# One decoder layer with attention, pooling and a 64-expert MoE: the per-layer projection takes the place of shared-expert products in the wait for the routing

## The reference, cut to what matters

```python
x = x + merged @ w_out
h2 = rmsnorm(x, g_ffn)
idx, wts = route(h2, w_router, router_bias)                  # 8 of 64 experts for a token
moe = routed_experts(h2, idx, wts, w_exp_gate, w_exp_up, w_exp_down) \
    + swiglu(h2, w_sh_gate, w_sh_up, w_sh_down)              # the shared expert, width 256
x = x + moe
ple_gate = sigmoid(rmsnorm(x, g_ple) @ w_ple_gate)
x = x + ple_gate * rmsnorm(p @ w_ple_proj, g_ple_post)       # p: 512 x 256, w_ple_proj: 256 x 1024
```

## Time and profile before

| | us |
|---|---|
| device time, median of 3 runs (lowest to highest) | 989.55 (988.99 to 990.61) |
| span of the profiled execution, first to last instruction | 986.4 |
| median less that span | 3.15 |
| PE busy / DVE / POOL / ACT in the span | 932.8 / 360.1 / 226.8 / 162.6 |
| PE: idle ahead of `up` / of `down`, in all | 26.1 / 3.1 |
| bytes moved by DMA, mean rate | 301.04 MB, 305 GB/s |

### The profile page before, as it was taken

How to read it: one execution, slowest core, us unless ns; L and a number is a source line. 1 busy time by engine, 2 the same in 40 slices (tenths; PEclk the granted TensorE clock), 3 DMA queues, 4 the chain that set the end, 5 groups by cost and what they waited for, 6 DMA issues and landing times.

```text
span 986.4 us, 15652 instructions
## 1 busy us (share of the span) xinstructions
PE 932.8 (95%) x6359; PEld 483.9 (49%) x6359; DVE 360.1 (37%) x773; ACT 162.6 (16%) x304; POOL 226.8 (23%) x344
## 2 busy tenths in 40 slices
PE   6999999999999999999999999989979889897798
PEld 4678788888655533333333333344323333332344
DVE  5565673336436733333332110111101111111687
ACT  2001324210011211111111111111101102121021
POOL 4115923162100112222222222212121211201110
PEclk9999999999999999999999999999989999999899
DMA  9940005421482699999999999999999999999972
GB/s 331 331 129 1 1 1 184 158 86 63 143 317 107 223 385 386 407 418 395 411 420 407 398 422 410 408 422 415 397 422 421 421 421 419 419 401 373 380 270 85
DMA packets 83912, 301.04 MB, mean 305 GB/s; under 512 B 9299, under 2 KB 35959, under 8 KB 59648
## 3 DMA queue, kind: packets, MB, share of 16 engines
q1 hardware_dynamic: 70144, 263.19, 67.8%
q0 software_dynamic: 11920, 33.63, 8.8%
q10 hardware_dynamic: 1776, 3.21, 0.9%
HBM read 279.26 MB, written 29.36 MB: 313 GB/s over the span
## 4 chain that ended last, share of the span: by engine, by line
PE 74%; DMA 20%; SPq 2%; DVE 2%; issue 1%; ACT 1%; POOL 0%; ACTq 0%; POOLq 0%
PE ps L2223 22%; DMA ring<-in_w_exp_up 18%; PE ps L1826 12%; PE ps L2252 8%; PE ps L1976 6%; PE ps L1955 5%; PE ps L2367 4%; PE ps L1782 3%; PE ps L1759 2%; PE ps L2047 1%; PE ps L1788 1%; DMA ring<-accumulator 1%; PE ps L2232 1%; DMA accumulator<-actT,stage 1%; SPq L525 1%; PE ps L1875 1%
## 5 line engine op out<-in xcount | busy, mean ns | idle before, releaser
L2223 PE MATMUL ps<-ring,gates 128*32 128x512 f32 x2560 | 289.3, 604 | 26.1 <-DMA ring<-in_w_exp_up 25.3
L2223 PEld LDWEIGHTS ps<-ring,gates 128*32 128x32 f32 x2560 | 88.8, 111 | 218.6 <-issue 217.7
L2252 PE MATMUL ps<-ring,poolbuf 128*32 128x512 f32 x1280 | 145.6, 595 | 3.1 <-DMA ring<-in_w_exp_down 3.1
L1573 DVE COPY poolbuf<-ps 128x256 f32<-128x256 f32 x40 | 17.0, 424 | 355.4 <-PE ps L2232 355.4
L791 POOL TENSOR_TENSOR tickets<-cst 128x1 f32<-128x1 f32 x77 | 14.5, 188 | 397.1 <-ACT actT L991 391.7
L2252 PEld LDWEIGHTS ps<-ring,poolbuf 128*32 128x32 f32 x1280 | 37.9, 109 | 83.5 <-issue 81.9
L991 ACT ACTIVATE actT<-ps,qT 128x1024 f32<-128x1024 f32 x40 | 44.5, 1113 | 142.3 <-PE ps L2252 142.3
L983 ACT ACTIVATE poolbuf<-ps 128x256 f32<-128x256 f32 x40 | 15.4, 384 | 280.0 <-PE ps L2223 280.0
L1826 PE MATMUL ps<-xrow,ring 128*128 128x256 f32 x256 | 57.9, 381 | 0.1
L1976 PE MATMUL ps<-ring,gates 128*128 128x512 f32 x128 | 56.4, 594 | 0.0
L1759 PE MATMUL ps<-cst,rows 128*128 128x128 f32 x352 | 47.6, 281 | 8.3 <-DVE rows L1087 8.3
(11 more groups left out here) (294 smaller groups left out, 1062.3 us busy)
## 6 DMA issues: line engine op xcount, KB each, us to landing
ring<-in_w_exp_down SPq DMA_DIRECT2D x64, 1024.0 KB, 17.6
ring<-in_w_exp_gate SPq DMA_DIRECT2D x62, 1024.0 KB
ring<-in_w_exp_up SPq DMA_DIRECT2D x62, 1024.0 KB
ring<-accumulator SPq DMA_DIRECT2D x12, 1024.0 KB, 13.1
ring<-in_w_gate SPq DMA_DIRECT2D x8, 1024.0 KB, 13.2
ring<-in_w_in SPq DMA_DIRECT2D x5, 1024.0 KB, 12.9
xrow<-in_x SPq DMA_DIRECT2D x8, 512.0 KB, 5.1
accumulator<-ring SPq DMA_DIRECT2D x1, 4096.0 KB, 19.9
```

Source lines behind the costliest of these rows:

```text
L2223: last = mm(bank(2 + k)[part, :], hgT[k][:, q, part], pair_view(EXPERT_SLOT[js[c]])[:, q], start=(q == 0), stop=(q == KD - 1))
L2252: last = mm(bank(6 + half)[part, :], eactT[r % 2][:, q, part], w[:, q, half * 512:(half + 1) * 512], start=(q == 0), stop=(q == 1))
```

## The change

1. `shared_up` is gone. In its places PE runs `ple_proj(m0, m1)`: the 16 products of 128x512 of `p @ w_ple_proj`, in the same pieces. They need six banks (`PLE_BANK`), and eight pairs of ACT instructions empty them: a copy to `pp` and a square with its sum (`ple_evict`).
2. The shared gate and up products of all four tiles are jobs: eight `late_T` and four `late_up` in steps 24 to 29, `shared_T` in 30, `shared_down` in 33 to 36. `ple_proj` and `ple_square` are no jobs any more; `ple_gain` (DVE, now from SBUF) is in steps 16 to 23.
3. The shared gate and up weights are loaded once, in four halves of 0.5 MiB. `w_ple_proj` is a dense unit in slot 8. Gate and up of expert 3 are loaded with the first experts, its down weights (slot 8) after the last `ple_proj`. `w_sh_down` is loaded in two halves after step 31.
4. `rows_T(0)`, `up(1)` and the first `silu` wait for `ple_squared`; `down(0)` and `up(1)` no longer wait for `shared_act`.

The core of the diff; renumbered jobs, the views of the buffers and `late_up`, whose body is as before but for the place of its weights, are left out.

```diff
@@ -54,9 +54,10 @@
-LATE = (2, 3)
+UPS = 3 * NT
...
-JOB_STEP = [SMALL_AT + n // 2 for n in range(8)] + [SMALL_AT + 6 + n // 2 for n in range(4 * NT)]
+JOB_STEP = [SMALL_AT + n // 2 for n in range(UPS + 2)] + [SMALL_AT + 9 + n // 2 for n in range(2 * NT)]
+GAIN_AT = NGROUP
@@ -148,14 +149,15 @@
-    ["wa0", "wa1", "wb0", "wb1"] + [f"out{c}" for c in range(4)] + ["shg", "shu"]
-DENSE_SLOT = [u % 8 for u in range(13)] + [8, 9, 10, 11] + [1, 2, 3, 4, 6, 7]
+    ["wa0", "wa1", "wb0", "wb1"] + [f"out{c}" for c in range(4)] + ["ple"]
+DENSE_SLOT = [u % 8 for u in range(13)] + [8, 9, 10, 11] + [1, 2, 3, 4] + [8]
...
+PLE_TILE = [3, 2, 0, 1]
+PLE_BANK = [7, 3, 0, 1, 7, 3, 7, 4]
@@ -506,14 +508,12 @@
...
             sp.wait_ge(merged_ready, 4)
-            for u in range(DENSE_AT["shg"], N_DENSE):
-                load_dense(u)
@@ -552,36 +552,36 @@
+            def load_shared(n):
+                w = t["w_sh_gate" if n < 2 else "w_sh_up"][0].rearrange("(k p) n -> p k n", p=P)
+                sp.dma_start(sh_late[n], w[:, 4 * (n % 2):4 * (n % 2) + 4, :]).then_inc(sh_late_loaded, 16)
             load_in(0, 0)
+            load_dense(DENSE_AT["ple"])
             load_down(0, 0)
             load_part(1, 1, 0)
...
-            load_down(3, 3)
+            load_in(3, 3)
             sp.wait_ge(x1_ps, 2 * NT - 1)
...
             sp.wait_ge(x1_ps, 2 * NT)
             load_in(2, 2)
+            sp.dma_start(gpost, t["g_ple_post"].broadcast_to([P, D])).then_inc(gpost_loaded, 16)
+            load_shared(0)
             sp.wait_ge(logit_ps, NT)
-            sp.wait_ge(pT_ps, 2)
-            sp.wait_ge(sel_ready, NT)
-            sp.wait_ge(gathered[0], 16)
-            sp.dma_start(shg_late, unit_source("shg")).then_inc(sh_late_loaded, 16)
-            for c in range(2):
-                sp.dma_start(shu_late[c], unit_source("shu")[:, 4 * c:4 * c + 4, :]).then_inc(sh_late_loaded, 16)
-            sp.dma_start(gpost, t["g_ple_post"].broadcast_to([P, D])).then_inc(late_loaded, 16)
-            sp.wait_ge(shared_ps, 2)
-            load_in(3, 3)
+            load_shared(1)
+            sp.wait_ge(ple_ps, 2 * NT)
+            load_down(3, 3)
+            load_shared(2)
             sp.wait_ge(order_ready, 1)
-            def load_ple_proj():
-                sp.wait_ge(tokw_ready, 1)
-                for j in range(2):
-                    sp.dma_start(w_ple[j], t["w_ple_proj"][0][j * P:(j + 1) * P, :]).then_inc(late_loaded, 16)
...
-                sp.dma_start(w_shd, t["w_sh_down"][0].rearrange("(j p) n -> p j n", p=P)).then_inc(late_loaded, 16)
+                for j in range(2):
+                    sp.dma_start(w_shd[j], t["w_sh_down"][0][j * P:(j + 1) * P, :]).then_inc(sh_late_loaded, 16)
@@ -594,7 +594,8 @@
                     in_used(step)
...
-                        load_ple_proj()
+                        sp.wait_ge(tokw_ready, 1)
+                        load_shared(3)
@@ -613,7 +614,7 @@
-                    if step == SMALL_AT + 2:
+                    if step == SMALL_AT + 6:
@@ -962,13 +963,27 @@
+            def ple_evict(n):
+                i, half = PLE_TILE[n // 2], n % 2
+                act.wait_ge(ple_ps, n + 1)
+                nc.scalar.activation(pp[:, i, half * 512:(half + 1) * 512], bank(PLE_BANK[n]), ACT.Copy
+                                     ).then_inc(ple_copied, 1)
+                if n >= 3:
+                    act.wait_ge(ple_squared, n - 2)
+                nc.scalar.activation(ple_junk[n % 3], bank(PLE_BANK[n]), ACT.Square,
+                                     accum_out=st[:, 2, 2 * i + half:2 * i + half + 1]).then_inc(ple_squared, 1)
+            for n in range(3):
+                ple_evict(n)
@@ -980,6 +995,8 @@
+                if r == 0:
+                    act.wait_ge(ple_squared, 2 * NT)
@@ -990,26 +1007,18 @@
-            def ple_square(n):
...
-            shared_silu_of(0)
+                if n < UPS and n % 3 == 2:
+                    shared_silu_of(n // 3)
+            ple_evict(3)
+            ple_evict(4)
...
             rows_hi(0, 0)
-            shared_silu_of(1)
+            for n in range(5, 2 * NT):
+                ple_evict(n)
@@ -1591,12 +1598,13 @@
...
-                    dve.wait_ge(late_loaded, 64)
-                dve.wait_ge(ple_squared, n + 1)
...
-                                        gpost[:, half * 512:(half + 1) * 512], ALU.mult).then_inc(ple_copied, 1)
+                    dve.wait_ge(gpost_loaded, 16)
+                    dve.wait_ge(ple_copied, 2 * NT)
...
+                nc.vector.tensor_tensor(own, own, gpost[:, half * 512:(half + 1) * 512], ALU.mult
+                                        ).then_inc(ple_copied, 1)
@@ -2009,45 +2017,48 @@
...
-            def shared_up(i, k0, k1):
-                if i == 0 and k0 == 0:
-                    loaded("shg")
-                    loaded("shu")
-                w = pair_view(DENSE_SLOT[DENSE_AT["shg"]])
-                for k in range(k0, k1):
-                    last = mm(bank(SH_BANK[i]), actT[:, k, i * P:(i + 1) * P], w[:, k], start=(k == 0),
...
-                if k1 == KD:
-                    last.then_inc(shared_ps, 1)
+            def ple_proj(m0, m1):
+                for m in range(m0, m1):
+                    n, j = m // 2, m % 2
+                    i, half = PLE_TILE[n // 2], n % 2
+                    if m == 0:
+                        loaded("ple")
+                        pe.wait_ge(pT_ready, 2)
+                    if m == 2:
+                        pe.wait_ge(h2T_ready, 2 * NT)
+                    if m == 4:
+                        pe.wait_ge(ssq2_done, NT)
+                    if j == 0 and n in (4, 5, 6):
+                        pe.wait_ge(ple_squared, (1, 2, 5)[n - 4])
+                    last = mm(bank(PLE_BANK[n]), pT[:, j, i * P:(i + 1) * P], w_ple[:, j, half * 512:(half + 1) * 512],
+                              start=(j == 0), stop=(j == 1))
+                    if j == 1:
+                        last.then_inc(ple_ps, 1)
@@ -2086,9 +2097,9 @@
-            shared_up(0, 0, 1)
+            ple_proj(0, 1)
             router(3, 1)
-            shared_up(0, 1, 6)
+            ple_proj(1, 6)
@@ -2098,7 +2109,7 @@
-            shared_up(0, 6, 7)
+            ple_proj(6, 7)
@@ -2117,7 +2128,7 @@
-            shared_up(0, 7, 8)
+            ple_proj(7, 8)
@@ -2127,14 +2138,14 @@
-            shared_up(1, 0, 2)
+            ple_proj(8, 10)
             pe.wait_ge(maskedT_ready, 2)
...
-            shared_up(1, 2, 4)
+            ple_proj(10, 12)
@@ -2194,7 +2193,7 @@
-                    pe.wait_ge(ssq2_done, NT)
+                    pe.wait_ge(ple_squared, 4)
@@ -2203,7 +2202,7 @@
-                    pe.wait_ge(shared_act, 2)
+                    pe.wait_ge(ple_squared, 2 * NT)
@@ -2255,19 +2253,17 @@
...
             rows_T(0)
-            shared_up(1, 4, 8)
+            ple_proj(12, 16)
```

More of the change, by code:

```diff
@@ L325, in build @@
             sem("ple_ps"), sem("ple_squared"), sem("ple_copied"), sem("ple_rstd"))
+        ple_junk = [poolbuf[:, E0 + k * 512:E0 + (k + 1) * 512] for k in range(3)]
         logit_ps, scores_ready = sem("logit_ps"), sem("scores_ready")
@@ L508, in _ @@
             sp.dma_start(y_rows[0], zero_row.unsqueeze(1).broadcast_to([P, TOPK, D])).then_inc(y_first, 16)
-            for u in range(8, DENSE_AT["shg"]):
+            for u in range(8, DENSE_AT["ple"]):
                 load_dense(u)
@@ L970, in shared_silu_of @@
                 act.wait_ge(shared_ps, i + 1)
-                nc.scalar.activation(sh_row[:, i, :], bank(SH_BANK[i])[:, 0:FE], ACT.Silu,
+                act.wait_ge(ple_copied, 4 * NT)
+                nc.scalar.activation(sh_row[:, i, :], bank(5)[:, 0:FE], ACT.Silu,
                                      scale=st[:, 1, i:i + 1]).then_inc(shared_silu, 1)
@@ L1617, in _ @@
                 for n in jobs_of(r, 0) + jobs_of(r, 1):
-                    if n < 6 and n % 3 < 2:
+                    if n < UPS and n % 3 < 2:
                         late_T(n // 3, n % 3)
[L1620 to L1625, removed]
-                    else:
-                        ple_gain(n - 8 - 2 * NT)
+                    elif n < UPS:
+                        shared_mult(n // 3)
+                    elif n < UPS + 2:
+                        shared_T(n - UPS)
+                    else:
+                        base(n - UPS - 2)
+                if GAIN_AT <= r < GAIN_AT + 2 * NT:
+                    ple_gain(r - GAIN_AT)
             act_T(STEPS - 1, (STEPS - 1) % 2)
@@ L2010, in rank, with late_T @@
                 mm(at, triT[:, :], selb[:, i * NE:(i + 1) * NE], start=(i == 0), stop=True).then_inc(rank_ps, 1)
-            def late_T(c, half):
-                i = LATE[c]
-                if c == 0 and half == 0:
+            def late_T(i, half):
+                if i == 0 and half == 0:
                     pe.wait_ge(list_ready, NGROUP)
@@ L2024, in late_T @@
                 last.then_inc(h2T_ps, 1)
[L2026 to L2031, removed]
```

(43 more changed lines are left out.)

53 lines of the change are left out of this document (16 added, 37 removed).

## The result

| | us |
|---|---|
| device time before, median of 22 runs (lowest to highest) | 989.24 (986.28 to 991.84) |
| device time after, median of 22 runs (lowest to highest) | 991.09 (988.96 to 993.8) |
| after to before, with its 95% interval | 1.0018 (1.0011 to 1.0026) |
| span of the profiled execution, before / after | 986.4 / 987.2 |
| bytes moved by DMA, before / after | 301.04 / 298.96 MB |

The change moves 2.08 MB less and is 0.18% slower, 1.8 us. The forecast was 989.5 us and no change; the median lies inside the range, but the loss is beyond noise.

A forecast was written before the change was run, and what follows sets the result against it. PE was taken to set the pace from 342.6 to about 555 us, transfers after that. All terms summed to 0: 986.4 + 3.15 gives 989.5 us; own range 988 to 991.3, 8-in-10 range 986.0 to 991.6 us.

The forecast's parts named there:

- the 1.5 MiB from 320 to 337 us: Loads added while the last `h2` rows are stored: could delay store and first gather 0 to 3.9 us; taken as 0.
- the end: Steps 37 to 39 without jobs: PE idles some 5 us ahead of `up(38)`, scatter 1.7 us later; taken as 0, kept 0 to 1.7.
- PE's fill of the routing: `ple_proj` replaces 16 shared products of the same shape in the routing, ACT emptying banks in time: 0.
- The table load: Silu table load moves to step 0's silu, runs before its wait, is over by 345.5: 0.
- rival C: Step 0: the table load lies behind the silu's wait, costing 1.28 us, 990.8 us; chance 0.07.
- The 3.67 MB taken out ahead of 371 us: 3.5 MiB fewer loads from 337 to 364 us, 9.0 us at 407 GB/s; worth 0, SP's queue being empty before 371.47.
- rival A: Lead of transfers survives past 371.47: waits after 559 us shrink by up to 9.0 us, 980.5 us, `up(31)` before 752; chance 0.17.
- Steps 28 and 29: With new jobs 19.5 us each against 17.37 us of transfers, eating 2.1 us of backlog each; queue doesn't run dry: 0.
- rival B: Steps 28 and 29 starve the queue: 4.2 us lost with no backlog, 993.7 us, DMA share below 0.95 from 720 to 750; chance 0.10.
- PE's waits for the up weights: Sign in the profile after: still some 25 us, moved away from steps 28 and 29 to steps 37 and 38.
- `up(17)` within 1 us of 547: Sign in the profile after: the start of step 17's `up` stays within 1 us of 547.
- 200 us in which PE sets the pace: Stretch between the idle queue and the transfer-bound steps; claimed to speak against a lead of the transfers paying.

The follow-up runs named there:

- run 4: Changed kernel with expert 1's up and down weights (2 MiB) loaded 9 us later, ahead of the first gather: 995.9 us, 1.006 to the kernel before.
- run 2: Changed kernel with the eight `shared_down` one step later, in steps 34 to 37: 990.89 us, 1.001 to the kernel before.
- run 5: Kernel before, with its eight `shared_down` and eight `ple_proj` one step earlier, so step 37 has no jobs: 989.84 us, 1.0011.
- run 3: Changed kernel with `gpost` and two gate halves behind the first gather and `shared_down` in steps 34 to 37: 989.86 us, 0.9998 to the kernel before.
- run 6: run 3's kernel with `pp` kept in bf16, `w_sh_down` in the freed place but still loaded after step 31: 989.67 us, 1.0002 to the kernel before.
- Runs 8 and 9: run 6's kernel with `w_sh_down` (1 MiB) loaded before 371 us, timed twice: 987.25 us, 0.9988, and 986.94 us, 0.9974, to the kernel before.
- run 9: Second timing of run 6's kernel with `w_sh_down` loaded before 371 us: 986.94 us, 0.9974 to the kernel before.

## Why the prediction was wrong, step by step

**The step that failed first: the 1.5 MiB from 320 to 337 us.** The prediction wrote that the store "is on ACT's queue and the gather on POOL's, so neither stands behind SP's. I take 0 and keep 3.9 as an end." That they are on other queues is no shelter: the store landed 3.9 us later, as long as these bytes take at 407 GB/s, and the first gather was released by it. (That the two agree is no rule: run 4 had 2 MiB more in flight, and its store took only 1.0 us more.) Part of that was slack (before, the gather's list was the later one, and PE had work up to 338.19); some 1.2 of the 1.44 us by which `up(0)` is late came from it, and some 1.2 us reached the end. The Trainium skill, "DMA: Bandwidth & Descriptors", Issuing engines are not separate DMA queues, says that transfers started by any engine run on the same 16 DMA engines and interleave; the landing times of 3.7, 7.6 and 8.6 us agree. The value taken was wrong, and the end of 3.9 us, though named, was left out of the forecast's own range, which took in 1.7 us above: the store's own row, 3.7 us with 2 MiB issued ahead of it, did not show what it would take with 3.5 MiB.

**The step that failed second: the end.** "So `down(37)` and its scatter can come 1.7 us later. The loads that follow stand in a queue that the transfers fill, so I take 0 and keep 0 to 1.7." The scatter came 3.6 us later, of which 2.9 were the slower `up(38)`: the 1.7 us had been taken from the one row with 4.04 us of idle time (8.77 us), and after 4.9 to 5.0 us the runs show 8.55 to 9.95. And the queue was not full: the loads of the sums wait for this very scatter. Cost: 0.8 us in the changed kernel (run 2), 1.1 us in the kernel before (run 5), inside the 0 to 1.7 that were named.

**What held.** PE's fill of the routing cost nothing: no product waited for ACT. The table load ran at 345.39, 4.58 us of idle time ahead of step 0's silu, so rival C is out; the trace has it at 1.28 us and not behind the wait:

```profile
345.39 1.28 ACT L1000 ACT_TABLE_LOAD   x1
351.25 0.38 ACT L1000 ACTIVATE poolbuf<-ps 128x256 f32<-128x256 f32 x1 [4.58 <-PE ps L2222]
```

The 3.67 MB taken out ahead of 371 us gave nothing, since the queue was empty there in both kernels; rival A is out for this change (24.1 us of waits, `up(31)` at 753.87, not before 752). Steps 28 and 29 took the 19.5 us that were worked out, with a DMA share of 1.01 from 720 to 750: rival B is out. PE's waits for the up weights nearly kept their sum (25.3 and 24.1 us), but moved to steps 32, 33 and 38, not to 37 and 38. The sign "`up(17)` within 1 us of 547" failed with `up(0)`: 548.44.

**The sum, corrected:** 0 + 1.2 (gather) + 0.8 (end) = 2.0 us; measured 1.8, and 0 with both losses undone (run 3, and its control, run 6: 1.0002). The two terms are best values, each with more than 1 us of uncertainty. Both terms had been named with their bounds and set to 0 because they lay beside other work; in both the cover was looked for in SP's queue, and the wait was on a single transfer or scatter that others wait for. One premise of the sum was wrong without moving it: of the 3.15 us between span and median not all lie around the span. In every later execution the time is some 1.8 us above its span (988.98 against 987.2 in the changed kernel), so the first profile was of an execution some 1.3 us faster than the median, by this estimate.

**One reading stays open.** The prediction had two reasons for why the 3.67 MB gain nothing: the queue was empty before the release near 371 us, and a lead would be lost over "200 us in which PE sets the pace". The first is shown, before and after, and is enough: SP had nothing that it could issue into the holes before a step released a slot. The second no run tests. Runs 8 and 9 show something else: a byte taken out of the late steps, where the transfers bound, is worth its time, and the holes ahead of 371 us have room for it. The Trainium skill, "Perfetto Trace Analysis", Optimization Strategy, says that interleaving regimes can pay; runs 8 and 9 agree with it, the change itself shows that bytes must really be moved across, and not only be left out.

## What to carry to other kernels

A transfer that shares no queue with the loads you move earlier can still be slowed by them, here by 3.9 us: look for the one small store or gather in that stretch on which a chain waits, and don't price its delay at nothing. The time of the bytes added beside it was the right price for 1.5 MiB here, and far too much for the 2 MiB more of run 4. Where a kernel is bound by transfers from some point on and the queue runs empty ahead of it, as here, a byte saved ahead gains only if a byte from behind takes its place; ask what could be loaded there and what room it needs. Work taken out of the last steps leaves an engine idle just before the step on whose result the end waits; check what the idle time does to that step.

## What the runs showed of the hardware

- The same 512 KB store took 3.7, 7.6 (7.2 and 7.4 in two further profiles) and 8.6 us from issue to landing, with 2, 3.5 and 5.5 MiB of other loads issued on another queue in the 5 us before it.
- An idle PE paid twice. After 3.23 us of waiting the next 16 instructions, `rows_T(0)` and four products, ran 2.8 us longer, at a granted clock of 0.61 on the mean; after 4.92 to 5.01 us of waiting `up(38)` took 8.55 to 9.95 us instead of 7.07. After 1.31 us it took 7.08. What was lost did not grow with the wait: after 7.19 us `up(33)` of the changed kernel took 8.63, after 4.01 us `up(29)` of run 5 took 9.87, and after 2.73 us `up(33)` of run 9 took 7.07.
- Executions of one kernel differ by 2 to 3 us either way (986.28 to 991.84 in the kernel before), and a part of that can come in from the transfers in the middle of the steps: in the two profiles of the changed kernel `up(0)` started 0.14 us apart, but `up(18)` at 560.42 without a wait in the one and at 562.45 after 2.24 us of waiting in the other.
